# Wider down products, one-pass mask matmuls, and modulation panels moved from the mixers into the feed-forward stages

## The reference

```
for l in range(2):                                   # first block: 6 stages
    mod = (silu(c) @ w_ada[l] + b_ada[l]).reshape(B, 3, 3, 1024)
    x = x + 0.5 * gate(0) * swiglu(norm_mod(x, 0), w_ffn_up[l, 0], w_ffn_down[l, 0])
    x = x + gate(1) * mixer(norm_mod(x, 1), ...)     # RG-LRU, stick-breaking and forgetting attention
    x = x + 0.5 * gate(2) * swiglu(norm_mod(x, 2), w_ffn_up[l, 1], w_ffn_down[l, 1])
# second block: 4 stages, twice (mixer, swiglu); its mixer holds pooling, chunk attention,
# top-64 sparse attention and latent attention; then a last RMS norm

def norm_mod(h, j): return rms(h) * g_norm[l, j] * (1 + scale_j) + shift_j
def swiglu(h, w_up, w_down):                         # 1024 -> 2 x 2816 -> 2816 -> 1024
    g, u = split(h @ w_up); return (silu(g) * u) @ w_down
```

## Time and profile before

| | |
|---|---|
| median of 3 runs | 1713.06 us (1709.82 to 1714.77) |
| the profiled execution, and its span | 1709.39 us, 1707.6 us |
| TensorE busy | 1635.3 us, 96% of the span |
| VectorE busy | 1313.3 us, 77% |
| ScalarE busy | 913.9 us, 54% |
| DMA, mean over the span | 236 GB/s |

### The profile page before, as it was taken

The page is one execution under the profiler, slowest core; times in us unless marked ns, Lnnn a source line. Parts: engine busy times, 40 slices in busy tenths (PEclk is TensorE's granted clock), DMA queues, the critical chain, the costliest instruction groups (busy, mean ns, idle before and its releaser), DMA issues.

```text
span 1707.6 us, 31946 instructions
## 1 busy us (share of the span) xinstructions
PE 1635.3 (96%) x13290; PEld 1604.8 (94%) x13290; DVE 1313.3 (77%) x2071; ACT 913.9 (54%) x1564; POOL 84.0 (5%) x124
## 2 busy tenths in 40 slices
PE   2999999999999999999999999979999999899998
PEld 2999998999999999998999999978999998899998
DVE  6688898788788878897788888847888898385553
ACT  5445458664445544477554545646545456464453
POOL 4000000000000000000110001001000010010000
PEclk8999999999999999999999999989999999999999
DMA  9787765348786778754378888313778773145451
GB/s 357 301 317 300 300 253 198 124 178 336 294 317 261 300 300 316 290 210 173 115 271 312 305 318 301 124 50 117 301 300 319 296 250 124 50 149 197 176 196 50
DMA packets 57168, 403.22 MB, mean 236 GB/s; under 512 B 6606, under 2 KB 6866, under 8 KB 9280
## 3 DMA queue, kind: packets, MB, share of 16 engines
q1 hardware_dynamic: 55424, 396.01, 61.6%
q0 software_dynamic: 1600, 5.18, 1.0%
HBM read 400.10 MB, written 1.05 MB: 235 GB/s over the span
## 4 chain that ended last, share of the span: by engine, by line
PE 81%; DVE 11%; ACT 4%; issue 2%; DMA 1%; SPq 0%; DVEq 0%; ACTq 0%
PE PS L507 81%; DVE WL L1602 3%; DVE SCR L1602 2%; DVE SCR L1605 1%; ACT WH L1146 1%; DVE ring L1629 1%; ACT SCR L1429 1%; DMA SCR<-in_x 1%; DVE X L1605 1%; DVE HL L1605 1%; DVE SCR L1599 1%; DVE SMALL L1984 1%; DMA ring<-in_win 0%; ACT HH L1178 0%; DVE SCR L1946 0%
## 5 line engine op out<-in xcount | busy, mean ns | idle before, releaser
L1602 DVE TENSOR_TENSOR WL<-ring,WH 128x1024 fp32r<-128x1024 f32 (+1 forms) x508 | 599.8, 1215 | 187.4 <-ACT WH L1146 186.8
L507 PE MATMUL PS<-HH,WH 128*128 128x256 f32 (+1 forms) x2640 | 651.5, 285 | 12.7 <-ACT WH L1146 9.5
L507 PE MATMUL PS<-HL,WH 128*128 128x256 f32 (+1 forms) x2640 | 640.1, 283 | 0.0
L1146 ACT ACTIVATE WH<-ring 128x1024 fp32r<-128x1024 f32 (+1 forms) x508 | 510.9, 1048 | 100.1 <-PE PS L507 39.7
L507 PEld LDWEIGHTS PS<-HH,WH 128*128 128x128 f32 x2640 | 497.2, 190 | 18.8 <-ACT WH L1146 9.7
L507 PEld LDWEIGHTS PS<-HL,WH 128*128 128x128 f32 x2640 | 495.1, 190 | 0.7
L507 PE MATMUL PS<-HH,WL 128*128 128x256 f32 (+1 forms) x2640 | 375.9, 280 | 2.3 <-DVE WL L1602 2.2
L507 PEld LDWEIGHTS PS<-HH,WL 128*128 128x128 f32 x2640 | 339.4, 189 | 3.7 <-DVE WL L1602 3.7
L1629 DVE CUSTOM_DVE_ANT_0 ring<-ring,CB,VC 128x1024 f32<-128x1024 f32 x240 | 316.4, 1339 | 9.0 <-DMA ring<-in_ada 8.9
L507 PE MATMUL PS<-AH,WH 128*128 128x256 f32 x1056 | 297.5, 282 | 0.0
L507 PE MATMUL PS<-AL,WH 128*128 128x256 f32 x1056 | 297.0, 281 | 0.0
(11 more groups left out here) (206 smaller groups left out, 1488.0 us busy)
## 6 DMA issues: line engine op xcount, KB each, us to landing
ring<-in_up SPq DMA_DIRECT2D x88, 1024.0 KB, 5.6
ring<-in_ada SPq DMA_DIRECT2D x72, 1024.0 KB, 7.2
ring<-in_ffn SPq DMA_DIRECT2D x66, 1024.0 KB, 4.8
ring<-in_mod SPq DMA_DIRECT2D x48, 1024.0 KB, 6.9
ring<-in_down SPq DMA_DIRECT2D x44, 1024.0 KB, 6.5
ring<-in_win SPq DMA_DIRECT2D x32, 1024.0 KB, 6.9
ring<-in_wout SPq DMA_DIRECT2D x16, 1024.0 KB, 4.8
ring<-in_winv SPq DMA_DIRECT2D x4, 1024.0 KB, 4.8
```

The lines of the kernel that those rows point to most:

```text
L507: return e.matmul(out, lhsT, rhs, start=start, stop=stop, skip_group_check=skip)
L1146: e.activation(half_of(i)[0], slot_of(("unit", u))[:, w * (i % 2):w * (i % 2) + w], ACT.Copy).then_inc(s_hi, 1)
L1602: return e.tensor_tensor(out, a, b, op)
```

## The change

There are four parts.

1. In the down product `AH` and `AL` of one hidden tile now lie side by side (`AHL`), and for chunks 0 to 6 one matmul of 512 columns takes the place of the two of 256 that had the same weights. The two sums stand in the two halves of the bank, and `residual` adds them to `X` in two steps, one after the other. Chunk 7 stays as it was.
2. The mask matmuls take rounded (fp32r) operands: copies of the identity and of two masks, written by three ScalarE instructions in stage 0, and the selection, which VectorE now writes rounded (`WKR`). The constant `BIG` is a power of two.
3. `ADA_N` goes from (21, 3, 20, 20, 3, 20, 3, 20, 2, 0) to (22, 2, 20, 21, 0, 22, 0, 21, 0, 4). In stage 9 the panels stand in the ticks of the hidden tiles.
4. The constants are laid out in another order; transposes read the identity through the rounded copy.

```diff
@@ -55,7 +55,7 @@
 FIRST_ADA = 8
-ADA_N = (21, 3, 20, 20, 3, 20, 3, 20, 2, 0)
+ADA_N = (22, 2, 20, 21, 0, 22, 0, 21, 0, 4)
 NADA = 120
...
@@ -77,7 +77,9 @@
     if SUBS[n][0] == "ffn":
-        at = [q for q in halves if 3 + q * (NTICK["ffn"] - 3) // len(halves) == t]
+        ticks = NF - 3 if n == NSUB - 1 else NTICK["ffn"] - 3
+        at = [q for q in halves if 3 + q * ticks // len(halves) == t]
     else:
...
@@ -112,8 +118,9 @@
         SCR = sb("SCR", [128, SCR_N])
-        AH = nc.alloc_sbuf_tensor_at("AH", [128, NF, S], F32R, offset=scr_at)
-        AL = nc.alloc_sbuf_tensor_at("AL", [128, NF, S], F32R, offset=scr_at + 4 * NF * S)
+        AHL = nc.alloc_sbuf_tensor_at("AHL", [128, NF, 2, S], F32R, offset=scr_at)
+        AH, AL = AHL[:, :, 0, :], AHL[:, :, 1, :]
...
@@ -674,11 +685,15 @@
                     out = PS[:, banks[c % len(banks)], 0:256]
-                    mm(out, wh[:, g, :], xh(k), start=k == 0, stop=False)
-                    mm(out, wh[:, g, :], xl(k), start=False, stop=False)
+                    if c < KD - 1:
+                        both = PS[:, banks[c % len(banks)], :]
+                        mm(both, wh[:, g, :], AHL[:, k, :, :].rearrange("p a s -> p (a s)"), start=k == 0, stop=k == kt - 1, skip=True)
+                    else:
+                        mm(out, wh[:, g, :], AH[:, k, :], start=k == 0, stop=False)
+                        mm(out, wh[:, g, :], AL[:, k, :], start=False, stop=False)
                     if g == 0:
                         e.wait_ge(s_lo, h + 1)
-                    last = mm(out, wl[:, g, :], xh(k), start=False, stop=k == kt - 1)
+                    last = mm(out, wl[:, g, :], AH[:, k, :], start=False, stop=k == kt - 1, skip=c < KD - 1)
                     if g == 7:
...
@@ -793,8 +808,8 @@
                         mm(c[:, 128:256], nones, s_[:, 256:384], start=False, stop=False, skip=True)
-                        last = mm(v3(c, 3)[:, 0:3:2, :], ident,
-                                  const("sbpos").rearrange("p (o k) -> p o k", o=1).to_broadcast([128, 2, 128]),
+                        last = mm(v3(c, 3)[:, 0:3:2, :], identr[:, :],
+                                  sbposr[:, :].rearrange("p (o k) -> p o k", o=1).to_broadcast([128, 2, 128]),
                                   start=False, stop=True, skip=True)
...
@@ -969,7 +984,7 @@
                         per = 512 // m
-                        mm(s3[:, h:h + per, :], ident, WK[t][:, 0:m].rearrange("p (o k) -> p o k", o=1).to_broadcast([128, per, m]),
+                        mm(s3[:, h:h + per, :], identr[:, :], WKR[t][:, :].rearrange("p (o k) -> p o k", o=1).to_broadcast([128, per, m]),
                            start=True, stop=False, skip=True)
...
@@ -1224,6 +1240,9 @@
                         e.activation(CB[:, 1, :], CB[:, 1, :], ACT.Silu).then_inc(s_cb, 1)
+                        e.wait_ge(s_const_rest, 16)
+                        for exact, k in ((identr, "ident"), (causalr, "causal"), (sbposr, "sbpos")):
+                            e.activation(exact[:, :], const(k), ACT.Copy).then_inc(s_exact, 1)
                     if f >= 3:
...
@@ -1688,8 +1707,10 @@
                 e.wait_ge(*summed(n, c))
-                banks = (4, 5, 0, 1, 2, 3)
-                stt(X[:, c, :], PS[:, banks[c % 6], 0:256], MOD[:, 24 * n + 16 + c:24 * n + 17 + c], X[:, c, :], ALU.mult,
+                b = (4, 5, 0, 1, 2, 3)[c % 6]
+                if c < KD - 1:
+                    step(stt(X[:, c, :], PS[:, b, 256:512], MOD[:, 24 * n + 16 + c:24 * n + 17 + c], X[:, c, :], ALU.mult, ALU.add))
+                stt(X[:, c, :], PS[:, b, 0:256], MOD[:, 24 * n + 16 + c:24 * n + 17 + c], X[:, c, :], ALU.mult,
                     ALU.add).then_inc(s_x, 1)
...
@@ -1949,7 +1970,7 @@
                     step(tt(wk, wk, SC[t][:, 0:m], ALU.not_equal))
-                    ts(wk, wk, BIG, -BIG, ALU.mult, ALU.add).then_inc(s_sel, 1)
+                    ts(WKR[t][:, :], wk, BIG, -BIG, ALU.mult, ALU.add).then_inc(s_sel, 1)
...
```

More of the change, by code:

```diff
@@ L18 @@
 EPS = 1e-6
-BIG = 1.0e30
+BIG = 2.0 ** 100
 LOWEST = -3.0e38
@@ L35, in columns @@
     return out, at
-CONST_SPEC = [("ident", 128), ("ones", 128), ("eps", 1), ("one", 1), ("bd", 128), ("ntri", 128), ("partner", 96), ("rev", 128), ("cos", 256), ("sin", 256),
+CONST_SPEC = [("bd", 128), ("ntri", 128), ("partner", 96), ("rev", 128), ("cos", 256), ("sin", 256),
               ("cnt", 512), ("causal", 128), ("nones", 128), ("chunk", 256), ("sbpos", 128), ("sb01", 128),
-              ("onehot", 320)]
+              ("onehot", 320), ("ident", 128), ("ones", 128), ("eps", 1), ("one", 1)]
 CONST, NCONST = columns(CONST_SPEC)
-FIRST = CONST["bd"]
+FIRST = CONST["ident"]
 VEC_SPEC = [("gfinal", 8), ("t5", 4), ("lam", 8)]
@@ L104, in build @@
         SQ = sb("SQ", [128, KD, S])
+        cn_at = nc.sbuf_base
         CN = sb("CN", [128, NCONST])
+        identr, causalr, sbposr = (nc.alloc_sbuf_tensor_at(k + "r", [128, 128], F32R, offset=cn_at + 4 * CONST[k])
+                                   for k in ("ident", "causal", "sbpos"))
         VC = sb("VC", [128, NVEC])
@@ L175, in build @@
         eps = const("eps")
+        ident1 = identr[:, :].bitcast(F32)
         one = const("one")
@@ L276, in build @@
         SC = [scr(128), scr(256)]
+        wk_at = scr_at + 4 * Scratch.at
         WK = [scr(128), scr(256)]
+        WKR = [nc.alloc_sbuf_tensor_at(f"WKR{t}", [128, 128 * (t + 1)], F32R, offset=wk_at + 512 * t) for t in range(2)]
         CQ = v3(scr(512), 2)
@@ L405, in _ @@
                 if p == 14:
-                    e.dma_start(CN[:, FIRST:], A["consts"][:, FIRST:]).then_inc(s_const_rest, 16)
+                    e.dma_start(CN[:, 0:FIRST], A["consts"][:, 0:FIRST]).then_inc(s_const_rest, 16)
             for g in range(2):
@@ L648, in turned_back @@
                 for t in range(2):
-                    last = e.transpose(PS[:, (6 if c < 4 else 0) + t, 128 * (c % 4):128 * (c % 4) + 128], XG[:, c, 128 * t:128 * t + 128], ident)
+                    last = e.transpose(PS[:, (6 if c < 4 else 0) + t, 128 * (c % 4):128 * (c % 4) + 128], XG[:, c, 128 * t:128 * t + 128], ident1)
                 if c % 4 == 3:
@@ L659, in token_sums, with out_proj @@
                     last.then_inc(s_fss, 1)
-            def out_proj(n, xh, xl, ready):
+            def out_proj(n, ready):
                 kt = depth_of(n)
@@ L749, in fox_score @@
                     for h in range(0, 4, per):
-                        mm(s3[:, h:h + per, 128 * t:128 * t + 128], ident,
-                           causal.rearrange("p (o k) -> p o k", o=1).to_broadcast([128, per, 128]), start=True, stop=False, skip=True)
+                        mm(s3[:, h:h + per, 128 * t:128 * t + 128], identr[:, :],
+                           causalr[:, :].rearrange("p (o k) -> p o k", o=1).to_broadcast([128, per, 128]), start=True, stop=False, skip=True)
                     for h in range(4):
@@ L767, in fox_turn @@
                         for h in range(4):
-                            last = e.transpose(PS[:, 6 + r % 2, 128 * h:128 * h + 128], softmax_of(t)[:, h, 128 * kt:128 * kt + 128], ident)
+                            last = e.transpose(PS[:, 6 + r % 2, 128 * h:128 * h + 128], softmax_of(t)[:, h, 128 * kt:128 * kt + 128], ident1)
                         last.then_inc(s_atr, 1)
@@ L901, in index_rows @@
                     for t in range(2):
-                        last = e.transpose(PS[:, 7, 128 * t:128 * t + 128], SKI[:, 128 * t:128 * t + 128], ident)
+                        last = e.transpose(PS[:, 7, 128 * t:128 * t + 128], SKI[:, 128 * t:128 * t + 128], ident1)
                     last.then_inc(s_savt, 1)
@@ L1113, in _ @@
                     e.wait_ge(s_const_rest, 16)
+                    e.wait_ge(s_exact, 3)
                 if kind == "mix1":
```

10 lines of the change are left out of this document (5 added, 5 removed).

## The result

In alternating runs on one chip the changed kernel took 1707.35 us in the median (20 runs, 1705.57 to 1716.0) and the kernel before 1712.89 (20 runs). The ratio is 0.997, 95% interval 0.9962 to 0.9978: 5.1 us less, 3.8 to 6.5. A second timing beside the experiments gave 0.9987 (0.9976 to 0.9997), 2.2 us less, 0.5 to 4.1; the two intervals just overlap. The forecast was 21.5 us less and a range of 1682 to 1704; the time lies above the range. The mixers gave about what was forecast. The down products, the largest term, gave nothing and then cost something.

What follows compares the result with a forecast made beforehand. TensorE, busy for 96% of the span and carrying 81% of the chain, was taken as the bound. Terms -13.9 + 3.0 - 4.6 - 3.6 - 2.4 = -21.5 us gave 1691.6 us as the median, range 1682 to 1704.

Steps and rivals of the forecast that it cites:

- Down products, TensorE: Down products of six stages: 924 matmul pairs of 235 ns become one of 220, saving 13.9 us, bounds 17.6 and 0.
- Rival 1: Down products: time belongs to the columns, a 512-column matmul takes twice 117.5 ns, gain 0; 1702.5 us, chance 0.14.
- the forecast's own signs of being wrong: Tile at 353 or more, TensorE gaps behind weight splits, down-product clock below 1.00, or mixers 6 and 8 shorter by whole panels.
- Stage 9: Last down product: 2.3 us faster on TensorE, no VectorE loss, its four added panels costing nothing.
- Down products, VectorE: Down products: second adds and added half panels use up VectorE's room, 3.0 us lost, between 0 and 9.
- the lead of 1.5 to 2: Down products: how many us VectorE works ahead and can be late before TensorE waits.
- Masks, first kind: Mask matmuls in two mixers: rounded operands take 0.9 us instead of 3.5 each; 4.6 saved, bounds 3 and 5.2.
- Masks, second kind: Selection's second mask in two mixers: 1.25 to 2.5 us saved each, 1.8 taken, 3.6 for two.
- Panels: Mixer 4: its second panel moved away saves 2.4 us, bounds 0 and 4.2; the other panel moves nothing.
- Rival 2: VectorE or the ring takes over: five of six down products keep their 62 us; 1700, far end 1704, chance 0.11.
- Rivals 3 and 4: 512-column fp32r misses the one-pass rate, 1884 us, chance 0.04; rounded masks keep two passes, 1700 us, chance 0.03.

Runs made afterwards that it cites:

- Experiment 6: Changed kernel without the second add, its wide matmul set to 512, 384, 256, 192, 128 or 64 columns by stage; only steps read, no time.
- experiment 4: Changed kernel without the second add of seven chunks in each down product, TensorE's matmuls kept; 1701.23 us, ratio 0.9948.
- experiment 5: Kernel before with the wide down product and its second add alone, masks and panels as before; 1712.88 us, ratio 0.9998.
- experiment 3: Changed kernel with the panels placed as before the change; 1705.09 us, ratio 0.9966.
- experiment 8: Changed kernel with 256-wide down products and stage 9's four panels spread over stages 0, 3, 5 and 7; 1709.22 us, ratio 0.9989.

## Why the prediction was wrong, step by step

- **Down products, TensorE: -13.9. This is the step that failed.** "The upper is cost by columns alone, 235 ... I take 220, near the 216 of the row with the same stream." Measured 235, so 0.0 a pair. The error was to take the stream time of a rounded matmul from fp32 records (0.42 ns a column step) where 256 rounded columns stood at 0.459 in the same trace. That the step stays at 116 with weights of four columns showed that the weight load was not the 9 ns; it did not show that an instruction had an overhead. Experiment 6 finds none: 64 columns take 29 ns. Rival 1, at 0.14, had this step right, though not the time: its 1702.5 leaves out what VectorE then lost. Two of the forecast's own signs of being wrong are in the trace, a tile at 353 and gaps on TensorE behind the weight splits. The section "Back-to-back issue gap" of "TensorE: Matmul & The Clock Gate" in the Trainium skill, named beside the rival, speaks for it in form: nearly all by columns. Its size for 256 columns, 109 ns (given there for a matmul by itself), does not agree with the 117.5 here, nor its 216 for 512 with the 235. By its formula a pair would save 2.5 ns and the change 2.3 us, an estimate, where the prediction has 2.6 and 2.4.
- **Stage 9** was to gain 2.3 us and lost 1.0 in the trace (74.7 against 73.7). All of it is the step: in four chunks the kernel before ran at 340 ns a tile, and every later version, with 256 columns too, at 353. Beside that the stage has two lengths by chance: the granted clock falls in its last chunk in some traces (0.79 from 1690 to 1698 us in both kernels' traces) and not in others, and without the fall the changed kernel's stage took 72.9.
- **Down products, VectorE: +3.0, bounds 0 and 9.** Measured 3.8 or 6.7 by ratio (experiment 4 against the changed kernel) and 6.4 and 6.2 in two traces, within the bounds, but by luck. The sum took 2.3 us a stage off VectorE's room because TensorE would be faster, and TensorE was not. Without these the same sum leaves +1.7 in stage 2, +0.4 in stages 0, 3 and 7 and -0.8 in stage 5, less than the lead of 1.5 to 2 everywhere: no loss at all. Two things in it failed. It counted VectorE's idle time over the whole down product, while the lead has its low points at a few chunks: 0.8 us in stage 0 and 1.5 in the others before the change, and the idle time elsewhere doesn't help there. And "the first wait for them is ScalarE's, which has room, so I add nothing for it" left out that such a wait goes on to VectorE and TensorE once the lead is short, as after the 5.01 us in stage 0. The loss needs both, second adds and added half panels: second adds alone lost nothing by the ratio (experiment 5) or 0.4 us in two stages (experiment 3).
- **Masks, first kind: -4.6.** The one of 512 and the two of 256 columns took 0.65 us together where 0.22 + 2 by 0.12 = 0.46 had been forecast and 1.84 stood before. Mixers 1 and 4 became 1.9 and 3.0 us shorter by the masks alone (with their layouts), 4.9. Right.
- **Masks, second kind: -3.6.** 4.2 and 4.4 by the traces of masks alone. Right in sum, with some luck. From the second mask to the next stretch mixer 6 saved 0.8 and mixer 8 1.7, where 1.8 each had been forecast with 1.25 as the lower bound: the clock did give part back, in mixer 6 more than half. The rest, 0.3 and 0.1 ahead of the mask and 0.7 and 0.75 behind the scores, was forecast as nothing. In the changed kernel mixer 6 has 0.9 ahead of the mask (84.46 us became 83.56), 0.6 at it (7.12 became 6.49) and 0.9 behind (50.76 became 49.85). The wide product alone shows no such gain behind the scores (50.75), so it belongs to the masks and what came with them; the cause stays open.
- **Panels: -2.4.** 1.6 and 3.0 by ratio without the wide product, the uncertainty of each about 2. In mixer 4 the 2.0 us wait went as forecast; its length fell by 0.5 us in one pair of traces and by 2.5 in the other. In agreement without the wide product, as far as that uncertainty lets one say; with it, the same panels lost at least as much in the down products as they won.
- **Rival 2** named the engine, but had five down products keep their 62 us; they took 62.45 to 64.60.
- **Rivals 3 and 4** did not come true: 512 columns run at the one-pass rate, and the masks are one pass.

The terms as measured, from ratios: masks -6.8, panels -2.3, wide product 0, and all together -5.1 or -2.2 instead of the -9.1 of that sum, so 4.0 to 6.9 lost between wide product and panels. The second add carries it, since without it -8.9 is left. Had the wide step alone been put at 235 and the 3.0 us left as they were, the forecast would have been 1705.5, 1.9 us short of what came.

What stays open: how much of the lead the panels take by their own 1.27 us each and how much by the loads that they hold up. The 5.0 us wait of the changed kernel and the 5.5 us one of experiment 8 point to the ring's loads; no run varied the ring's slots or the order of the loads alone.

## What to carry to other kernels

Before merging matmuls, find out whether their step is stream or overhead: divide the step by its columns at two widths of the same data type. A step per instruction can be merged away, a step per column can't, and a step measured on another data type answers neither. A merged result that must be added on another engine has its price there, and that price may show only when something else (here two half panels) fills the same stretch: time each edit of a bundle alone and beside the others. For an engine that works ahead of another, don't sum its idle time: read its lead at each hand-over and find the smallest, since new work is paid from that. In a ring shared by several kinds of loads, count when each consumer frees its slot, not only how busy the consumers are.

## What the runs showed of the hardware

- A rounded matmul streams at about 0.46 ns a column from 64 to 512 columns (29 ns for 64, 60 for 128, 235 for 512), with no overhead that shows, while an fp32 record of 256 columns takes 216 ns, 0.42 by column step if such a record is two passes.
- Matmuls with new weights of 128 by 128 did not follow each other faster than about 114 ns in the mean: a 256-column matmul took 197 ns behind one of 64, the two together 226, and float32 matmuls of one column stand 112 ns apart in the kernel before.
- The same 256-column step runs at 113 to 114 ns or at 117 to 118 in one run (stage 9 of the kernel before has both, 117.5 in its first three chunks and 113.5 in the next four). What switches it was not found; 512 columns stayed at 235.
- A shorter mask ahead of the scores left 4.3 us of these at 1.2 GHz in mixer 6 of the changed kernel, where behind the long one about 0.6 us ran so. It differs from run to run: mask and scores together took 7.1 and 6.8 us before, and 5.1 to 6.4 with the masks alone.
